# Expert rows in half-fixed packs that mix two experts by column groups, two convolution inputs moved behind the scan of the group before, and four idle products ahead of the first expert rows

## What is computed

```
def moe(h, router_w, router_b, w_gate, w_up, w_down):
    scores = jax.nn.sigmoid((t @ router_w).astype(F32))
    ...
    _, idx = lax.top_k(jnp.where(in_grp, biased, -jnp.inf), TOP_K)
    ...
    hg = jnp.einsum('td,edf->tef', t, w_gate)
    hu = jnp.einsum('td,edf->tef', t, w_up)
    act = jax.nn.silu(hg) * hu * gates[..., None].astype(t.dtype)
    out = jnp.einsum('tef,efd->td', act, w_down)
```

## Time and profile before

| | |
|---|---|
| median of 3 runs | 2040.35 us (2037.51 to 2043.9) |
| the profiled execution | 2038.09 us, of which the trace spans 2036.2 us |
| TensorE matmul busy | 1608.9 us (79%) |
| VectorE, ScalarE, GpSimd busy | 644.6, 567.5, 264.5 us |
| moved by DMA | 326.99 MB, mean 161 GB/s |

### The profile page before, as it was taken

The page is one execution under the profiler, slowest core; times in us unless marked ns, Lnnn a source line. Parts: engine busy times, 40 slices in busy tenths (PEclk is TensorE's granted clock), DMA queues, the critical chain, the costliest instruction groups (busy, mean ns, idle before and its releaser), DMA issues.

```text
span 2036.2 us, 17209 instructions
## 1 busy us (share of the span) xinstructions
PE 1608.9 (79%) x5763; PEld 852.0 (42%) x5763; DVE 644.6 (32%) x1045; ACT 567.5 (28%) x1111; POOL 264.5 (13%) x200
## 2 busy tenths in 40 slices
PE   3996899997549998169779879889879963899980
PEld 2443444443524443155345445444454433444430
DVE  2122566622300000323563563753750032000002
ACT  3002444411112221323353443542620010222211
POOL 0023000012300000400310310311210031000005
PEclk9998799998569999559989989989879975899995
DMA  9205445492179995331231231330260004799964
GB/s 363 84 0 154 162 170 186 161 293 72 48 280 345 357 350 208 104 96 49 94 93 41 93 95 40 113 114 0 90 251 0 0 11 167 279 357 351 355 243 155
DMA packets 192601, 326.99 MB, mean 161 GB/s; under 512 B 8962, under 2 KB 116946, under 8 KB 192534
## 3 DMA queue, kind: packets, MB, share of 16 engines
q1 hardware_dynamic: 173260, 270.29, 38.7%
q0 software_dynamic: 9232, 33.79, 4.6%
q10 hardware_dynamic: 10048, 22.19, 2.8%
HBM read 276.95 MB, written 49.28 MB: 160 GB/s over the span
## 4 chain that ended last, share of the span: by engine, by line
PE 57%; DMA 14%; issue 8%; DVE 7%; ACT 6%; POOL 5%; SPq 2%; ACTq 0%; DVEq 0%; POOLq 0%
PE ps L749 9%; PE ps L856 8%; PE ps L959 7%; DMA mem<-slot_rows 6%; PE ps L765 5%; DMA mem<-cum_rows 4%; PE ps L707 3%; PE ps L840 3%; PE ps L589 2%; PE ps L629 2%; PE ps L858 2%; PE ps L522 2%; PE ps L645 2%; PE ps L609 2%; DMA mem<-slot_rows,sloti 2%
## 5 line engine op out<-in xcount | busy, mean ns | idle before, releaser
L749 PE MATMUL ps<-mem 128*128 128x512 f32 x608 | 270.6, 598 | 0.0
L856 PE MATMUL ps<-mem 128*128 128x512 f32 x384 | 170.5, 597 | 2.5 <-ACT mem L1175 2.5
L1528 DVE TENSOR_TENSOR mem<-ps,mem 128x256 f32<-128x256 f32 x38 | 16.1, 425 | 490.5 <-ACT mem L1111 490.5
L749 PEld LDWEIGHTS ps<-mem 128*128 128x128 f32 x608 | 114.1, 193 | 129.4 <-issue 129.2
L840 PE MATMUL ps<-mem 128*128 128x512 f32 x320 | 149.2, 621 | 0.0
L765 PE MATMUL ps<-mem 128*128 128x512 f32 x304 | 138.6, 599 | 3.8 <-ACT mem L1115 3.8
L959 PE MATMUL ps<-mem 128*128 128x512 f32 x320 | 137.5, 592 | 0.0
L1583 DVE SCALAR_TENSOR_TENSOR mem<-mem 128x642 f32<-128x642 f32 x96 | 85.2, 888 | 138.7 <-ACT mem L1197 128.3
L741 PE MATMUL ps<-tab,mem 128*128 128x128 f32 x304 | 44.0, 292 | 88.3 <-DMA mem<-slot_rows 86.0
L589 PE MATMUL ps<-mem 128*128 128x512 f32 x240 | 107.1, 605 | 7.2 <-DMA mem<-in_attn_w_qkv 7.2
L513 PE MATMUL ps<-tab,mem 128*128 128x128 f32 x160 | 32.6, 378 | 99.6 <-DVE mem L1287 63.9
(11 more groups left out here) (284 smaller groups left out, 2277.7 us busy)
## 6 DMA issues: line engine op xcount, KB each, us to landing
mem<-in_mod_w SPq DMA_DIRECT2D x24, 2048.0 KB, 7.9
mem<-in_expert_w_gate SPq DMA_DIRECT2D x38, 1024.0 KB, 7.2
mem<-in_expert_w_up SPq DMA_DIRECT2D x38, 1024.0 KB, 10.7
mem<-in_expert_w_down SPq DMA_DIRECT2D x38, 1024.0 KB, 10.4
mem<-cum_rows SPq DMA_DIRECT2D x40, 512.0 KB, 4.3
mem<-slot_rows SPq DMA_DIRECT2D x38, 512.0 KB, 9.6
slot_rows<-mem ACTq DMA_DIRECT2D x38, 512.0 KB, 7.6
slot_rows<-mem SPq DMA_DIRECT2D x1, 13312.0 KB, 46.1
```

The lines of the kernel that those rows point to most:

```text
L749: last = nc.tensor.matmul(ps[:, 2 + j, :], XGT[j][:, k, :], WS[j][:, k, :], start=(k == 0), stop=(k == KD - 1))
L856: nc.tensor.matmul(ps[:, b, :], w[:, k, :], HT[:, k, SEQ:TOK], start=(k == 0), stop=(k == KD - 1))
```

## The change

Three changes are joined.

**Packs.** Expert e now owns the fixed slots 96e to 96e+95, so that 12 packs of 128 rows (`PACKS`) hold the first 96 rows of all the experts, whatever the routing. Each pack holds rows of two experts. Rows beyond 96 go to blocks of 64 (`EXTRA`), which a loop takes as packs of two blocks, four blocks in a trip; with the row counts above it is one trip (two packs) in each layer. In a pack each expert's rows are multiplied by its own weights, with output to its own range of PSUM partitions, which is a group of 32 or 64 columns of the array: `pack_parts` cuts packs 0, 3, 6, 9 into 64, 32, 32 columns, packs 1, 4, 7, 10 into 64, 64, and packs 2, 5, 8, 11 into 32, 32, 64. Weights have four buffers instead of two (`RING`), each expert is loaded once for its fixed rows and again for each block of extra rows, and since the first experts are known in advance, SP loads gate and up of experts 0 to 3 during the mixer's last stage and down of 0 to 2 by the time of the logits.

**Convolution inputs.** They come in the order x0, x1, B, C, x2, x3, and the first two of group g+1 stand behind chunks 3 and 4 of the scan of group g. The loop on TensorE is written out. ScalarE takes the last two gate products together.

**Idle products.** TensorE multiplies the identity by X four times, into a bank that nothing reads, when the scatter is done and ahead of the first rows.

```diff
+        def pack_parts(t):
+            out, r = [], 0
+            while r < P:
+                e = (P * t + r) // BASE
+                end = min(P, BASE * (e + 1) - P * t)
+                while r < end:
+                    w = 64 if r % 64 == 0 and end - r >= 64 else 32
+                    out.append((e, r, w))
+                    r += w
+            return out
...
-                first = [expert(j) for j in range(2)]
-                if l == 1:
-                    sp.wait_ge(ES["dn"], done * 2 + 1)
-                for j in range(2):
-                    load_in(first[j], j)
-                load_down(first[0], 0)
+                if l == 0:
+                    sp.wait_ge(s_wused[2], 11)
+                    load_in(0, 0)
+                    sp.wait_ge(s_oev, HALVES)
+                    load_in(1, 1)
+                    sp.wait_ge(s_op, NT)
+                else:
+                    sp.wait_ge(s_op2, NT)
+                    load_in(0, 0)
+                    load_in(1, 1)
+                    sp.wait_ge(s_op2, 2 * NT)
+                load_in(2, 2)
+                load_in(3, 3)
...
                 sp.wait_ge(ES["sc"], 2 * NT * 16 * (l + 1))
-                for j in range(2):
-                    load_rows(j, j)
+                for t in range(2):
+                    load_rows(t, t)
+                load_down(3, 3)
+
+                for step in range(-2, PACKS):
+                    if step + 4 < PACKS:
+                        sp.wait_ge(pk["xt"], d0 + (step + 3))
+                        load_rows(step + 4, step % 2)
+                    for e in range(RING, NE):
+                        if last_pack(e - RING) == step + 1:
+                            sp.wait_ge(pk["gu"], d0 + (step + 2))
+                            load_in(e, e % RING)
+                    for e in range(RING, NE):
+                        if last_pack(e - RING) == step:
+                            sp.wait_ge(pk["dn"], d0 + (step + 1))
+                            load_down(e, e % RING)
...
                     for k in range(KD):
-                        last = nc.tensor.matmul(ps[:, 2 + j, :], XGT[j][:, k, :], WS[j][:, k, :], start=(k == 0), stop=(k == KD - 1))
-                    last.then_inc(ES["gu"], 1)
+                        for m, c, w in parts:
+                            last = nc.tensor.matmul(ps[c:c + w, 2 + j, :], XGT[j][:, k, c:c + w], GUW[l][m][:, k, :],
+                                                    start=(k == 0), stop=(k == KD - 1))
+                    last.then_inc(pk["gu"], 1)
...
+                pe.wait_ge(ES["sc"], 2 * NT * 16 * (l + 1))
+                for k in range(4):
+                    nc.tensor.matmul(ps[:, 7, :], ident, X[:, k, 0:512], start=True, stop=True)
...
                     last.then_inc(s_yd, 1)
+                    if cc >= NT - 2 and g + 1 < SG:
+                        conv_input(g + 1, cc - (NT - 2))
```

More of the change, by code:

```diff
@@ L763, in down @@
+                def down(t, j, parts, loads):
+                    pe.wait_ge(pk["atc"], t + 1)
+                    for m, load in loads:
+                        pe.wait_ge(pk["ldn"][m], load * 16)
+                    if isn0(t):
+                        pe.wait_ge(pk["ycopy"], t)
                     for n in range(2):
                         for k in range(2):
-                            last = nc.tensor.matmul(ps[:, 5 + n, :], AT[j][:, k * P:(k + 1) * P], WD[j][:, k, n * 512:(n + 1) * 512],
-                                                    start=(k == 0), stop=(k == 1))
@@ L782, in moe @@
-                final = trips + done
-                act_turned(final, 0)
-                gate_up(final, 1)
-                down(final, 0)
-                act_turned(final, 1)
-                down(final, 1)
+                            for m, c, w in parts:
+                                last = nc.tensor.matmul(ps[c:c + w, 5 + n, :], AT[j][:, k * P + c:k * P + c + w],
+                                                        WD[m][:, k, n * 512:(n + 1) * 512], start=(k == 0), stop=(k == 1))
@@ new lines, in down, with ring @@
+                    last.then_inc(pk["dn"], 1)
+                def ring(t):
+                    parts = [(e % RING, c, w) for e, c, w in pack_parts(t)]
+                    loads = [(e % RING, w0 + (e // RING + 1)) for e in sorted({e for e, c, w in pack_parts(t)})]
+                    return parts, loads
+                w0 = 0 if l == 0 else pe.snap(trips_of(pe, 0) + NE // RING)
+                r0 = 0 if l == 0 else pe.snap(trips_of(pe, 0) + PACKS // 2)
+                pe.wait_ge(ES["sc"], 2 * NT * 16 * (l + 1))
@@ new lines, in moe @@
+                for k in range(4):
+                    nc.tensor.matmul(ps[:, 7, :], ident, X[:, k, 0:512], start=True, stop=True)
+                for t in range(-2, PACKS):
+                    if t + 2 < PACKS:
+                        rows_turned(d0 + (t + 2), t % 2, r0 + ((t + 2) // 2 + 1))
+                    if t >= 0:
+                        act_turned(d0 + t, t % 2)
+                    if 0 <= t + 1 < PACKS:
+                        gate_up(d0 + (t + 1), (t + 1) % 2, *ring(t + 1))
+                    if t >= 0:
+                        down(d0 + t, t % 2, *ring(t))
@@ new lines, in moe @@
+                pe.wait_ge(ES["np"], l + 1)
+                trips = trips_of(pe, l)
+                with pe.Fori(0, trips) as i:
+                    t = [pe.snap(i * 2 + d0 + PACKS), pe.snap(i * 2 + d0 + (PACKS + 1))]
+                    load = pe.snap(i + w0 + (NE // RING + 1))
+                    halves = [([(2 * j, 0, 64), (2 * j + 1, 64, 64)], [(2 * j, load), (2 * j + 1, load)])
+                              for j in range(2)]
+                    for j in range(2):
+                        rows_turned(t[j], j, pe.snap(i + r0 + (PACKS // 2 + 1)))
+                    for j in range(2):
+                        gate_up(t[j], j, *halves[j])
+                    for j in range(2):
+                        act_turned(t[j], j)
+                        down(t[j], j, *halves[j])
@@ new lines, in moe @@
+                trips = trips_of(act, l)
+                with act.Fori(0, trips) as i:
+                    t = [act.snap(i * 2 + d0 + PACKS), act.snap(i * 2 + d0 + (PACKS + 1))]
+                    for j in range(2):
+                        rows_out(t[j], j)
+                    for j in range(2):
+                        gate(t[j], j)
+                    for j in range(2):
+                        act_out(t[j], j)
+                        result_out(t[j], j, act.snap(i + s0 + PACKS // 2), i * 2 + (PACKS + j))
@@ L1738, in _ @@
                 last = nc.gpsimd.memset(KBD[g], 0.0)
-            last.then_inc(s_kz, 1)
+            last.then_inc(s_zero, 1)
             store_modulation(0, 1, 1)
```

406 lines of the change are left out of this document (213 added, 193 removed).

## The result

| | median | lowest to highest | ratio to before, 95% interval |
|---|---|---|---|
| before | 2042.12 us (4 runs) | 2037.51 to 2051.32 | |
| changed | 2127.34 us (4 runs) | 2125.45 to 2129.22 | 1.0419 [1.0392, 1.0446] |

The change makes the kernel 85 us slower. The forecast was 1932, in a range up to 2070. The profiled execution has a span of 2123.8 us, 87.6 more than before, so the two traces are compared by spans.

A forecast was written before the change was run, and what follows sets the result against it. It took the experts to be bound by DMA and TensorE at once. From the profiled 2038.1 us, -88 for the packs and -20 for the convolution inputs gave 1930, stated as 1932 for the median; range 1908 to 2070.

The forecast's parts named there:

- The packs' products: Experts' gate-up and down: unequal column groups run side by side, 12 packs need 140 us of TensorE, hidden under DMA.
- side by side at no cost: Mixed packs' products: column groups that don't touch overlap whatever their widths, a pack taking 11.7 us; the end chosen.
- one width after the other at 0.09 us a change: Mixed packs' products, the end not chosen: 64 and 32 columns take turns, each change of width costing about 0.09 us.
- rival 1: Experts' packs: widths don't mix, a mixed pack takes 23.9 us, the kernel about 2065 us, slower; chance 0.32.
- gate-ups of 15 us: Sign of being wrong: packs 0, 2, 3, 5 show gate-ups of 15 us, packs 1 and 4 of 7 us.
- DMA at 250 GB/s with TensorE never idle: Sign of being wrong, in the experts' packs: DMA slows to 250 GB/s while TensorE never idles.
- The convolution inputs: Scan stage: inputs inserted behind chunks start the third input 6.8 us earlier at three places, saving 20 us.
- about 9 us: Sign of being right, in the scan: the third convolution input follows a group's last L926 by about 9 us.
- The start of the packs: From last scatter to first gate-up: weights loaded during the mixer make it start 12 us earlier in both layers.
- the idle products themselves are now what ends last: Packs' start: rows land before the idle products end, at 573.0 and 1728.0 us.
- The bytes: Experts' loads and stores: 62 MiB remain per layer, 183 us, with additions 197 us; 88 us saved together with the earlier start.

The follow-up runs named there:

- run 1: The changed kernel with every part of a pack 32 columns wide: 1948.25 us, ratio 0.9536.
- runs 2 and 3: The changed kernel with mixed gate-ups reordered to one change of width instead of 15 (2094.31 us), then to eight (2117.48 us).
- Run 4: The changed kernel with ScalarE's copy of a turned input moved ahead of its copy of the next convolution input: 2080.83 us, ratio 1.0189.
- run 5: The kernel before with the scan part of the change alone: 2053.15 us; the same with ScalarE's copy of the turned input first: 2010.98 us.
- run 6: The changed kernel with 32-column parts and ScalarE's turned-input copy first: 1901.67 us; also without idle products: 1905.82 us; changed kernel only without idle products: 2128.90 us.
- Both mendings: The changed kernel with all parts 32 columns wide and ScalarE's copy of the turned input first: 1901.67 us, ratio 0.9282.

## Why the prediction was wrong

**The step that failed is the choice in "The packs' products".** It saw both ends, "side by side at no cost, and one width after the other at 0.09 us a change", and took the first. The runs show the second: with one width alone (run 1) the gate-up is 7.07 us, with two it is 15.95, and the turns make nearly all of the difference (runs 2 and 3). This was no unseen mechanism. It was rival 1, to which the text gave 0.32, and its signs ("gate-ups of 15 us", "DMA at 250 GB/s with TensorE never idle") are what the trace shows. The reason for choosing the other end was weak: L522's parts, of one width, show that the dispatch looks past a busy group, and this is true (the pair at 632.99), but all runs here show it only among products of one width. The Trainium skill, "TensorEngine Tiling (Array Packing)", section "Key Properties", says that changing the mode drains the engine; the alternation of the weight loads, 0.84 and 0.81 us idle ahead of each group, agrees. The one row of before with two widths near each other agreed too: its 0.52 us recur at every change here. With a page and a row for rival 1, and no row of two widths side by side against it, 0.32 was too little.

**Sizes within rival 1.** It gave 2065, and 2127 came. In the experts it was short by 23 us: a change costs 0.13 us and not 0.09, because the step behind it is longer too (0.46 or 0.48 us and not 0.43), so three packs take 60.7 us and not 59.5; and the two extra packs take 30.7 us instead of 25, since turnings and downs wait for ScalarE there (5.0 us of waits from 826 to 860 us). With the landing of the scatter this makes +44 and +25, where it had +31 and +13. The scan is short by 31 us, and the attention stage's 8 us of clock belong to no step.

**The convolution inputs.** "20 us", and the stage grew by 11. What was worked out of the insertion was right: the third input comes 8.7 us after the last chunk's end, as the forecast's sign says ("about 9 us"). The inserted input even ran at full clock, 8.7 us and not 11.1. What is missing is ScalarE: the text looked whether it could copy the first input in time, but not whether its copies of turned inputs come in time for the next turning. In the new order (x, x, B, C, x, x) the first three turnings stand behind three inputs in a row, and ScalarE's copy of each stands behind its copy of the input after it; in the old order an input without a turning or a gate product stood in between, and the wait was 6.0 us in the whole scan (4 times 1.5, at the old L874). Run 4 shows that this one position costs the 27.3 us and, by the clock, about 9 more; run 5 that without it the step is worth 30 us (19 to 42).

**The start of the packs.** "12 us earlier in both layers": 14.5 and 13.7 us from the last scatter's issue to the first gate-up, where before it was 26.0 and 26.1 (562.21 to 588.18 and 1717.23 to 1743.33); so 11.5 and 12.4 earlier. The scatter lands 4.8 us after its issue, not 2.9:

```profile
570.23 0.96 POOL L1873 DMA_INDIRECT slot_rows<-mem,sloti  x1 [0.30 <-issue]
575.04 0.82 SPq L422 DMA_DIRECT2D mem<-slot_rows  x2
575.07 6.58 PE L845 MATMUL ps<-mem,tab 128*128 128x512 f32 x8 [20.89 <-DMA slot_rows<-mem,sloti]
```

That "the idle products themselves are now what ends last" was right: without them the first turning starts 2 to 3 us earlier. What they give back is about what they cost, within 2 us a layer (run 6).

**The bytes.** With one width, the two stretches from scatter to last down are 45.3 and 61.9 us shorter than before, 107 together where 88 were forecast. The 197 us of a layer were 186 to 188, nearer to the bytes without additions.

Both mendings give 1902, 30 below the forecast of 1932. So all terms but two were right within 10 to 20 us, and these two decided: 179 us by the widths, 46 by one position in ScalarE's program (34 to 37 of them seen in the scan's trace). The 30 us below the forecast are the packs, which gave 19 us more, and the mended scan, some 10 more. What stays open is why the clock is granted differently in the same code at 240 us.

## What to carry to other kernels

- Groups of 64 and of 32 columns never ran side by side here, groups of one width did. Cut all parts of a pack to the smallest width that any of them needs: twice as many instructions cost nothing here (7.07 us against 7.09), a mixture doubled the time (15.95).
- When products are put in another order, walk through the program of every engine that serves them, in its order, and ask at each place what stands ahead of the instruction that TensorE needs next. A copy that is ready but stands behind a wait is late by that wait.
- Where two ends of an unknown cost lie 130 us apart and one row points to one of them, go with the row.

## What was unexpected in the hardware

- Products of one width overlap even over the border of two stages (down beside gate-up at 632.99), while a product of another width waits for its turn: 0.52 us to the next start instead of 0.43, and nothing beside it.
- 64 instructions of 32 columns take 7.07 us, 32 of 64 columns 7.09: the number of instructions doesn't count here.
- A wait of 3.4 us in a busy stretch can cost more than itself. Behind two of them the granted clock fell (0.80 from 1147 to 1172 us), and the inputs took 8.11 and 9.43 us instead of 7.03.
